# The norms between the blocks: turn and split of the second group of rows moved, weights' splits spread, the double norm's steps interleaved

## What is computed

```python
def layer_norm(x, g, b):
    mu = jnp.mean(xf, axis=-1, keepdims=True)
    var = jnp.mean(jnp.square(xf - mu), axis=-1, keepdims=True)
    return ((xf - mu) * lax.rsqrt(var + LN_EPS) * g + b)
def rms_norm(x, gain):
    y = xf * lax.rsqrt(jnp.mean(xf * xf, axis=-1, keepdims=True) + RMS_EPS)
    return y * gain
# first stack, three times in a layer
x = layer_norm(ALPHA * x + 0.5 * swiglu(x, w_in, w_out), g, b)   # or + mixer(x)
# second stack
xn = rms_norm(h, norm_mix[l]); h = h + mix(xn) @ w_out[l]
xn = rms_norm(h, norm_ffn[l]); h = h + (silu(g_ff) * u_ff) @ w_ffn_out[l]
```

## Time and profile before

| what | us |
|---|---|
| median of 3 runs | 3439.68 (3439.11 to 3440.82) |
| the profiled execution | 3442.97 |
| its span, first to last instruction | 3441.2 |
| TensorE busy | 3322.1 (97% of the span) |
| VectorE busy | 1480.4 (43%) |
| ScalarE busy | 1163.7 (34%) |
| GpSimd busy | 137.5 (4%) |
| granted TensorE clock, mean | 0.991 |

### The profile page before, as it was taken

One profiled execution on the slowest core, in us unless ns is written; L12 is line 12 of the kernel. 1 busy time (PEld: TensorE's weight loads), 2 busy tenths in 40 slices (PEclk: granted clock), 3 DMA queues, 4 the chain that ended last, 5 costly groups with the idle time before them and its releaser, 6 DMA issues. The chain is left out here.

```text
span 3441.2 us, 44909 instructions
## 1 busy us (share of the span) xinstructions
PE 3322.1 (97%) x18818; PEld 2748.5 (80%) x18818; DVE 1480.4 (43%) x2319; ACT 1163.7 (34%) x1955; POOL 137.5 (4%) x144
## 2 busy tenths in 40 slices
PE   8999999999999999989999898999999989999999
PEld 7888888888888888768888676778888766788887
DVE  3332544533253334335332565654332566553332
ACT  3221344322222222553222344443222344442221
POOL 0000111000000001000000100100000000000000
PEclk9999999999999999999999999999999999999999
DMA  4223222232323332112223221022223211122232
GB/s 164 95 98 116 88 76 72 88 98 98 110 86 98 98 104 95 56 50 87 94 95 116 81 92 56 32 68 96 96 94 108 99 62 56 38 86 99 98 102 70
DMA packets 88872, 302.51 MB, mean 88 GB/s; under 512 B 9504, under 2 KB 14880, under 8 KB 88672
## 3 DMA queue, kind: packets, MB, share of 16 engines
q1 hardware_dynamic: 88672, 299.64, 26.1%
HBM read 297.38 MB, written 2.23 MB: 87 GB/s over the span
## 5 line engine op out<-in xcount | busy, mean ns | idle before, releaser
L231 PE MATMUL ps<-xh,whi 128*128 128x512 f32 (+1 forms) x2664 | 1007.4, 378 | 28.3 <-DMA res<-in_tab 11.9
L232 PE MATMUL ps<-xl,whi 128*128 128x512 f32 (+1 forms) x2664 | 994.3, 373 | 0.0
L233 PE MATMUL ps<-xh,wlo 128*128 128x512 f32 (+1 forms) x2664 | 994.2, 373 | 0.0
L212 DVE TENSOR_TENSOR wlo<-raw,whi 128x1024 fp32r<-128x1024 f32 x535 | 647.3, 1233 | 635.5 <-ACT whi L204 635.1
L204 ACT ACTIVATE whi<-raw 128x1024 fp32r<-128x1024 f32 x535 | 547.5, 1050 | 503.9 <-PE ps L354 475.2
L231 PEld LDWEIGHTS ps<-xh,whi 128*128 128x128 f32 x2664 | 505.5, 190 | 135.4 <-issue 22.7
L233 PEld LDWEIGHTS ps<-xh,wlo 128*128 128x128 f32 x2664 | 505.9, 190 | 88.2
L232 PEld LDWEIGHTS ps<-xl,whi 128*128 128x128 f32 x2664 | 506.2, 190 | 84.3 <-issue 1.0
L698 DVE TENSOR_TENSOR tmp<-tmp,ps 128x512 f32<-128x512 f32 x132 | 90.7, 687 | 808.7 <-ACT tmp L683 741.9
L353 PE MATMUL ps<-wlo,hh 128*128 128x512 f32 x1056 | 415.7, 394 | 0.0
L352 PE MATMUL ps<-whi,hh 128*128 128x512 f32 x1056 | 415.2, 393 | 0.0
(11 more groups left out here) (313 smaller groups left out, 3319.7 us busy)
## 6 DMA issues: line engine op xcount, KB each, us to landing
raw<-in_w SPq DMA_DIRECT2D x535, 512.0 KB, 3.3
rows<-in_row SPq DMA_DIRECT2D x15, 512.0 KB, 4.7
xr<-in_xt SPq DMA_DIRECT2D x2, 1024.0 KB, 7.3
xr<-in_x SPq DMA_DIRECT2D x1, 2048.0 KB, 7.9
mn<-bounds SPq DMA_DIRECT2D x8, 256.0 KB, 4.6
out<-tmp SPq DMA_DIRECT2D x4, 256.0 KB, 3.0
out<-rows SPq DMA_DIRECT2D x4, 256.0 KB, 2.3
ntb<-in_tab SPq DMA_DIRECT2D x2, 320.0 KB, 4.2
```

The costliest lines, as they stand in the source:

```text
L212: v.tensor_tensor(self.wlo[u % NW][:, :], self.raw[u % NRAW][:, :], f32(self.whi[u % NW][:, :]), SUB).then_inc(*self.up("wlo", u))
L231: t.matmul(out, wh, xh, start=first, stop=False)
L232: t.matmul(out, wh, xl, start=False, stop=False)
L233: return t.matmul(out, wl, xh, start=False, stop=last)
```

## The change

The functions of a norm are cut finer, and the order is written out anew for three cases. What each instruction computes stays the same but for one step.
- TensorE: in norms without `then`, turn(1) moves from the middle of group 3's matmuls to their start. In norm 5 it stays.
- VectorE, norms 0 to 4 and 6 to 8: add(2), low(1), lo(end), scale(2), lo(end+1), add(3), lo(end+2), scale(3), lo(end+3), low(2), low(3).
- ScalarE there: root(0), root(1), high(0), root(2), high(1), hi(end), hi(end+1), root(3), hi(end+2), hi(end+3), high(2), high(3).
- Norm 5: the multiplication L492 moves from VectorE to ScalarE (`scaled_a`), ScalarE's squares and root of the second norm become `mean_a`, VectorE's reciprocal `root_v`, and all are placed among the other groups' steps.

```diff
@@ Norm.tensor
-                if i >= 2 and k == K - LAST and self.kind:
+                if self.kind and (i, k) in ((2, K - LAST), (3, K - LAST if self.then is not None else K - 2 * LAST)):
                     for j in range(2):
                         self.turn_t(t, i - 2, j)
@@ Norm.scale_v
-        if self.then is not None:
-            v.wait_ge(*c.at("nsd2", n, i))
-            v.reciprocal(st[:, 20:21], st[:, 19:20]).then_inc(*c.up("nrc", n, i, "rms"))
...
-            for h in range(2):
-                v.tensor_scalar(H(c.z[i % 2], h), H(x, h), st[:, 20:21], None, MULT).then_inc(*c.up("nz", n, i, h))
+    def root_v(self, v, i):
+        c, n, st = self.c, self.n, self.c.st[:, i, :]
+        v.wait_ge(*c.at("nsd2", n, i))
+        v.reciprocal(st[:, 20:21], st[:, 19:20]).then_inc(*c.up("nrc", n, i, "rms"))
@@ Norm.vector
+        elif self.then is None:
+            for i in range(4):
+                if i == 3:
+                    c.lo(v, self.end + 1)
+                self.add_v(v, 1, i)
+                if i == 2:
+                    self.low_v(v, 1)
+                    c.lo(v, self.end)
+                if i == 3:
+                    c.lo(v, self.end + 2)
                 self.scale_v(v, i)
                 if i == 1:
                     self.low_v(v, 0)
+            c.lo(v, self.end + 3)
+            self.low_v(v, 2)
+            self.low_v(v, 3)
+        else:
+            for i in range(4):
+                if i == 3:
+                    c.lo(v, self.end + 1)
+                self.add_v(v, 1, i)
+                if i == 1:
+                    self.root_v(v, 0)
                 if i == 2:
+                    self.low_v(v, 0)
+                    self.root_v(v, 1)
                     c.lo(v, self.end)
                     self.low_v(v, 1)
+                if i == 3:
+                    self.root_v(v, 2)
+                    c.lo(v, self.end + 2)
+                self.scale_v(v, i)
+            c.lo(v, self.end + 3)
             self.low_v(v, 2)
+            self.root_v(v, 3)
             self.low_v(v, 3)
@@ Norm: the rest of root_a for the double norm becomes mean_a(a, i), and
+    def scaled_a(self, a, i):
+        c, n = self.c, self.n
+        a.wait_ge(*c.at("nrc", n, i, "rms"))
+        if i >= 2:
+            a.wait_ge(*c.at("turn", n, i - 2, 1))
+        for h in range(2):
+            sl = slice(4 * P * h, 4 * P * h + 4 * P)
+            a.activation(c.z[i % 2][:, sl], c.xr[:, i, sl], COPY, scale=c.st[:, i, 20:21]).then_inc(*c.up("nz", n, i, h))
@@ Norm.scalar
+        elif self.then is None:
+            for i in range(4):
+                if i == 3:
+                    c.hi(a, self.end + 1)
+                self.root_a(a, i)
+                if i in (1, 2):
+                    self.high_a(a, i - 1)
+                if i == 2:
+                    c.hi(a, self.end)
+            c.hi(a, self.end + 3)
+            self.high_a(a, 2)
+            self.high_a(a, 3)
+        else:
+            for i in range(4):
+                if i == 3:
+                    c.hi(a, self.end + 1)
                 self.root_a(a, i)
                 if i == 1:
+                    self.scaled_a(a, 0)
+                    self.mean_a(a, 1)
+                if i == 2:
                     self.high_a(a, 0)
+                    self.scaled_a(a, 1)
+                    c.hi(a, self.end)
+                    self.high_a(a, 1)
+                    self.mean_a(a, 2)
+                if i == 0:
+                    self.mean_a(a, 0)
+                if i == 3:
+                    self.scaled_a(a, 2)
+                    c.hi(a, self.end + 3)
+                    self.high_a(a, 2)
+                    self.mean_a(a, 3)
+                    self.scaled_a(a, 3)
+                    self.high_a(a, 3)
```

More of the change, by code:

```diff
@@ L484, in scale_v @@
                                    op1=ADD).then_inc(*c.up("ny", n, i, h))
-        if self.then is not None:
-            v.wait_ge(*c.at("nsd2", n, i))
-            v.reciprocal(st[:, 20:21], st[:, 19:20]).then_inc(*c.up("nrc", n, i, "rms"))
-            v.wait_ge(*c.at("nrc", n, i, "rms"))
-            if i >= 2:
-                v.wait_ge(*c.at("turn", n, i - 2, 1))
-            for h in range(2):
-                v.tensor_scalar(H(c.z[i % 2], h), H(x, h), st[:, 20:21], None, MULT).then_inc(*c.up("nz", n, i, h))
+    def root_v(self, v, i):
+        c, n, st = self.c, self.n, self.c.st[:, i, :]
+        v.wait_ge(*c.at("nsd2", n, i))
+        v.reciprocal(st[:, 20:21], st[:, 19:20]).then_inc(*c.up("nrc", n, i, "rms"))
     def low_v(self, v, i):
@@ L518, in vector @@
                 self.add_v(v, 0, i)
[L519 to L523, removed]
+        if not self.kind:
+            for i in range(4):
[12 more added lines that the diff above has]
+                    c.lo(v, self.end + 2)
                 self.scale_v(v, i)
@@ L526, in vector @@
                     self.low_v(v, 0)
+            c.lo(v, self.end + 3)
[4 more added lines that the diff above has]
+                if i == 3:
+                    c.lo(v, self.end + 1)
+                self.add_v(v, 1, i)
+                if i == 1:
+                    self.root_v(v, 0)
                 if i == 2:
+                    self.low_v(v, 0)
+                    self.root_v(v, 1)
                     c.lo(v, self.end)
                     self.low_v(v, 1)
-        if self.kind:
-            c.lo(v, self.end + 2)
+                if i == 3:
[3 more added lines that the diff above has]
+            c.lo(v, self.end + 3)
             self.low_v(v, 2)
-            c.lo(v, self.end + 3)
+            self.root_v(v, 3)
             self.low_v(v, 3)
@@ L558, in root_a, with mean_a @@
         a.activation(st[:, 14:15], st[:, 13:14], SQRT, bias=c.col(V_EPS)).then_inc(*c.up("nsd", n, i))
[L559 to L568, removed]
+    def mean_a(self, a, i):
+        c, n = self.c, self.n
+        x, st = c.xr[:, i, :], c.st[:, i, :]
+        for h in range(2):
+            a.wait_ge(*c.at(*self.y_of(i, h)))
+            if h or i:
+                a.wait_ge(*c.at("nsq", n, 1 - h, i - 1 + h))
+            a.activation(c.tmp[4], x[:, 4 * P * h:4 * P * h + 4 * P], SQUARE, accum_out=st[:, 16 + h:17 + h]).then_inc(*c.up("nsq", n, h, i))
+        a.wait_ge(*c.at("nsq", n, 1, i))
+        a.activation(st[:, 18:19], st[:, 16:17], IDENT, bias=c.col(V_EPS + 1), scale=1.0 / D).then_inc(*c.up("nsq", n, "mean", i))
+        a.wait_ge(*c.at("nsq", n, "mean", i))
+        a.activation(st[:, 19:20], st[:, 17:18], SQRT, bias=st[:, 18:19], scale=1.0 / D).then_inc(*c.up("nsd2", n, i))
+    def scaled_a(self, a, i):
+        c, n = self.c, self.n
+        a.wait_ge(*c.at("nrc", n, i, "rms"))
+        if i >= 2:
+            a.wait_ge(*c.at("turn", n, i - 2, 1))
+        for h in range(2):
+            sl = slice(4 * P * h, 4 * P * h + 4 * P)
+            a.activation(c.z[i % 2][:, sl], c.xr[:, i, sl], COPY, scale=c.st[:, i, 20:21]).then_inc(*c.up("nz", n, i, h))
     def high_a(self, a, i):
@@ L602, in scalar @@
                 self.square_a(a, 0, i)
[L603 to L609, removed]
+        if not self.kind:
+            for i in range(4):
+                if i == 3:
+                    c.hi(a, self.end + 1)
+                self.copy_a(a, 1, i)
+        elif self.then is None:
+            for i in range(4):
+                if i == 3:
[9 more added lines that the diff above has]
+        else:
+            for i in range(4):
+                if i == 3:
+                    c.hi(a, self.end + 1)
                 self.root_a(a, i)
                 if i == 1:
+                    self.scaled_a(a, 0)
+                    self.mean_a(a, 1)
+                if i == 2:
                     self.high_a(a, 0)
[L613 to L619, removed]
+                    self.scaled_a(a, 1)
[4 more added lines that the diff above has]
+                    self.mean_a(a, 0)
+                if i == 3:
+                    self.scaled_a(a, 2)
[4 more added lines that the diff above has]
+                    self.high_a(a, 3)
     def pool_end(self):
```

## The result

The changed kernel takes 3450.77 us in the median of 9 runs (3446.14 to 3457.82), the kernel before 3439.68 in 9 runs on the same chip (3436.87 to 3443.32). The ratio is 1.0034, with a 95% interval of 1.0026 to 1.0043: **slower by 11 us**, 9 to 15 by the interval. The profiled execution took 3448.18 us with a span of 3446.4, 5.2 more than the span before. It lies 2.6 under its kernel's median, and the profiled one of before 3.3 above its own, so the trace shows less of the loss than the medians do.

A forecast was written before the change was run, and what follows sets the result against it. PE was taken as the bound, busy for 97% of the span, so only its waits could be won. Terms 11.2 (norms 0 to 4) + 0.6 (6, 8) + 5.1 (5) + 3.6 (7) = +20.5 us gave 3460.2 us, range 3441 to 3468.

The forecast's parts named there:

- The walk of norm 2: Step-by-step timing of norm 2 in the new order: lead 2.1 us sooner, turn(3) idle some 3.5 us, +3.4 us with a drop.
- Norms 0 to 4: Term for the five plain layer norms: +11.2 us together, or +3.7 with no clock drop at any of them.
- one drop more than before, at norm 2: Norm 2 kept its clock before; a 3.5 us idle at turn(3) should now drop it, +1.5 us.
- signs of being wrong: Turn(3) doesn't wait, the clock stays at 1.00 behind those waits, or L212 and L475 get in between GpSimd's instructions.
- Norms 6 and 8: No wait before; y(3) at 2339.7 where PE wants it at 2339.5: +0.3 us each, +0.6 together.
- it has to wait for the whole run, and I go by that: At norm 5, from one L492 of 3.84 us: VectorE is locked out until GpSimd's whole run of 5.5 us ends.
- Norm 5, +5.1: Double norm: last quarters end at 1983.0 against 1977.9, +5.1 us with lock and drop, upper end of -0.1 to +5.1.
- its own price of a drop: A fall of the clock after idle time costs some 1.5 us, worked out from norm 0's stretch against norm 2.
- Norm 7, +3.6: Scale(3) locked out by GpSimd's run until 2708.45, last quarters at 2717.9 against 2714.24: +3.6 us, bounds 0 and +4.8.
- the bound that I had set at 0 and not taken: At norm 7, without a lockout, the late unit covers all and the cost is 0.
- Rival 2: Group 3's norm is in time and both waits are simply gone: -27 us, 3412.5 us; chance 0.06.
- Rival 1: The wait moves to turn(3) cheaply, no drops beyond the old ones, no lock on runs: +4.2 us, 3443.9; chance 0.19.

The follow-up runs named there:

- e1: Changed kernel with the split of unit end+2 back behind scale(3) at the norms without `then`; 3442.1 us, ratio 1.0005 to the kernel before.
- e9: Changed kernel with ScalarE's copy of unit end+2 ahead of root(3) instead of behind it, at the norms without `then`; 3442.9 us in one run.
- e2: Changed kernel with norm 5 alone in the order of before; 3450.7 us, ratio 1.0033 to the kernel before.
- e11: Kernel before with norm 5 alone in the changed kernel's order; 3441.9 us, ratio 1.0003.
- e3: Kernel before with L492 as a product of two SBUF inputs instead of a product with a scalar; 3440.2 us, ratio 1.0003.
- e5: e4 with norm 5 ordered anew on ScalarE and VectorE and its turn(3) one quarter later; 3418.7 us, ratio 0.9943 to the kernel before.
- e4: Changed kernel, norms without `then`: add(3) before the end+1 split, end+2 copy before root(3), end+2 split after scale(3); 3430.8 us, ratio 0.9977 to before.

## Why the prediction came out as it did

**Direction and place: right.** Slower, with the time in the range, at the lower edge of the forecast's own band (3450 to 3467). The walk of norm 2 held step by step: the lead without a wait at 1001.9 in the time of before, 0.2 us for the split of `end+1` behind turn(2), seen on the weight loads (0.4 forecast), that split at 2.32 us, add(3) within 0.1 us, y(3) late, five waits at L408 for L483. They measured 3.28 us each where the text said 3.5. e1 and e9 showed the cause: 2.15 us were forecast for copy and split ahead of scale(3), and taking them away gave 2.08.

**Norms 0 to 4: +11.2 forecast.** By the medians it is +11.6 (e2 against before, with norms 6 to 8 in it), but two traces have less: +7.8 in the changed kernel's and, in e2's, +8.6. The match to 0.4 us is partly luck. Norm by norm the changed kernel's trace has +1.9 at norm 1 (2.1 forecast), +1.7 and +1.8 at norms 3 and 4 (1.9 each), +1.8 at norm 2 (1.9 without its drop, 3.4 with it) and only +0.65 at norm 0 (1.9), for which no reason was found. The forecast had one drop more than before, at norm 2. The traces don't: e2's has 0.50, 0.55, 1.00, 0.73 and 0.55 granted behind its five waits, norm 2 spared again. That the clock stays at 1.00 behind such a wait was one of the signs of being wrong, and at norm 2 it came. Norms 6 and 8 lost 0.07 us each in the trace, where 0.3 each was forecast.

**The size: 20.5 forecast, 11.1 measured.** Two terms were mis-sized, both by the same step, "it has to wait for the whole run, and I go by that": a VectorE instruction that meets GpSimd's run was taken to be locked out until its end, wherever in the run it falls. That L212 and L475 get in between GpSimd's instructions was a sign of being wrong as well, and it came.
- Norm 5, +5.1: measured 0 to 2.6. The step was placed wrongly before it was priced wrongly. I let GpSimd's run start at 1955.1, as soon as L638 ended. It waits for tables that SyncE issues at group 3's end, and group 3 ended late by the very wait at turn(1) that I had worked out; the run started 1.4 us later than I put it, and the split met its first group, where it was let in (1.23 us). Without the lock the same walk had all three turns within 0.5 us. The term also had a drop of 2.1 us behind turn(3), for which the text gives no row; its own price of a drop was 1.5.
- Norm 7, +3.6: measured 0, as far as the traces can tell (from norm 7's first turn to norm 8's, 371.9, 370.6 and 369.2 us in the old order of before, e11 and e3, 370.6 and 370.2 in the new one of the changed kernel and e2). The rows of the changed kernel are these, VectorE and GpSimd:

```profile
2708.35 1.51 DVE L212 TENSOR_TENSOR wlo<-raw,whi 128x1024 fp32r<-128x1024 f32 x1 [2.12 <-ACT whi L204]
...
2709.97 1.63 DVE L475 SCALAR_TENSOR_TENSOR tmp<-xr,st,rows 128x512 f32<-128x512 f32 x2
```
```profile
2708.31 3.60 POOL L2381 TENSOR_TENSOR nrk<-nga,ntr 128x128 f32<-128x128 f32 x4 [419.38 <-DMA nct<-in_tab]
```

  The split and L475 lie in the run's first group, and GpSimd was held up instead (3.60 for what takes 1.70). TensorE waited 0.2 us at turn(3), and the late unit `end+3` covered all, the bound that I had set at 0 and not taken.

The Trainium skill's rule (SBUF — State Buffer, section "SBUF: two separate sides"), one whole instruction at a time, by which I gave norm 5 +2.4, came closer to the time than my reading of the earlier trace rows. But it doesn't cover the whole record either: the lock-out for the rest of a run is real, and an L212 lost 1.8 us so in e3 and 3.4 in e5. Where in the run an instruction falls decides.

**The rivals.** Rival 2 (faster) was excluded by VectorE's own sum, and no turn(3) of norms 0 to 5 was in time in the changed kernel. It takes another order, e4, for that. Rival 1's price, +4.2, lies under the measured 9 to 15 us.

**Not settled.** Why VectorE is let in during the first four of GpSimd's products and not later. Whether norm 5's order costs 0 or 2.6 us. How much of the changed kernel's loss is drops: no run holds the clock fixed, and the traces show four drops of five at norms 0 to 4 both before and after.

## What to carry to other kernels

When a wait is removed from a hand-ordered chain, walk on to the next two points where the same engine is awaited: here 2 us were won at the lead and more was lost at the following turn, since an instruction with slack (a weight split for later) had been put ahead of one without. Ahead of an instruction that others wait for, put only what is needed sooner, and fill the time of its own latency (here the root on ScalarE) with work whose inputs are surely there. Work on GpSimd that can wait should be kept away from VectorE's critical stretch, even where it looks free.

## What the runs showed of the hardware

- **VectorE beside a run of GpSimd instructions.** Beside the first four of a run of twelve, VectorE's two-input instructions got in: seven L212 took 1.23 to 1.51 us (1.22 alone), a pair of products in e3 1.85, and in the changed kernel GpSimd's four took 2.71 and 3.60 us instead of 1.70. Beside the fifth and later ones VectorE got nothing until the run ended: eleven L212 in eight kernels, of 1.31 to 4.64 us, all ended 1.07 to 1.09 us after the run's last product. In the kernel before, one L492 took 3.84 us so.
- **Clock drops behind waits.** The granted clock of the 3.6 us behind the wait at norms 0 to 4 was 0.71, 0.54, 1.00, 0.72 and 0.57 behind 3.3 us (changed kernel); 1.00, 1.00, 0.63, 0.57 and 1.00 behind 1.8 to 1.9 us (e9); 1.00, 0.85, 0.77, 1.00 and 0.82 behind 1.2 us with one of 0.5 us close behind it (e1); 1.00 in all five behind 0.4 to 0.6 us (e4). From the lowest to the highest run the changed kernel spans 11.7 us (9 runs), e1 8.5 (11), e4 5.5 (9), but e2, with the changed kernel's waits, only 4.9 (6), so the spread alone doesn't show the drops.
- **A scaled copy on ScalarE** (L604, 128x512 in SBUF) takes 1.33 us for two, where VectorE's L492 takes 0.88 for two; the estimate was 0.6 each.
